# A two-layer hybrid encoder on one core: filler matmuls placed anew, ScalarE's drain points made finer, both layers written out

## Time and profile before

| | us |
|---|---|
| median of 3 runs (lowest, highest) | 3152.52 (3151.27, 3157.33) |
| the profiled execution's own time | 3157.31 |
| its span, first to last instruction | 3155.1 |
| TensorE busy | 2934.4 (93%) |
| VectorE, ScalarE, GpSimd busy | 1583.5, 970.8, 821.5 |
| mean granted TensorE clock | 0.97 of full |

### The profile page before, as it was taken

How to read it: one execution, slowest core, us unless ns; L and a number is a source line. 1 busy time by engine, 2 the same in 40 slices (tenths; PEclk the granted TensorE clock), 3 DMA queues, 4 the chain that set the end, 5 groups by cost and what they waited for, 6 DMA issues and landing times. The chain is left out here.

```text
span 3155.1 us, 46968 instructions
## 1 busy us (share of the span) xinstructions
PE 2934.4 (93%) x18888; PEld 1564.1 (50%) x18888; DVE 1583.5 (50%) x3180; ACT 970.8 (31%) x1836; POOL 821.5 (26%) x572
## 2 busy tenths in 40 slices
PE   6988999999998999999999889999999989999997
PEld 3445554566544465544445364545765444654443
DVE  2477867433379602155216877583334784020743
ACT  2245653211142324300113556522111432253000
POOL 1116312321243232232020353122211423322320
PEclk9998999999999999999999989989999999999998
DMA  5000101100111311263040011011011213112621
GB/s 203 17 27 14 54 14 41 38 32 29 45 64 31 112 65 46 94 206 110 0 141 17 27 37 31 14 40 41 29 32 52 67 38 119 54 44 94 227 77 60
DMA packets 132356, 195.87 MB, mean 62 GB/s; under 512 B 8072, under 2 KB 87976, under 8 KB 131880
## 3 DMA queue, kind: packets, MB, share of 16 engines
q1 hardware_dynamic: 113544, 158.74, 15.5%
q10 hardware_dynamic: 18592, 34.09, 2.9%
HBM read 146.14 MB, written 48.78 MB: 62 GB/s over the span
## 5 line engine op out<-in xcount | busy, mean ns | idle before, releaser
L493 PE MATMUL ps<-hT,wr 128*128 128x512 f32 x1600 | 768.5, 615 | 27.9 <-ACT wr L539 27.9
L493 PEld LDWEIGHTS ps<-hT,wr 128*128 128x128 f32 x1600 | 295.5, 196 | 342.7 <-issue 298.6
L493 PE MATMUL ps<-sums,wr 128*128 128x512 f32 x800 | 381.5, 605 | 3.8 <-ACT xo L548 3.8
L639 POOL TENSOR_TENSOR gts<-gts,wr 128x512 f32<-128x512 f32 x96 | 147.6, 1538 | 620.6 <-ACT wr L539 495.1
L493 PEld LDWEIGHTS ps<-sums,wr 128*128 128x128 f32 x800 | 146.8, 193 | 161.3 <-issue 152.1
L717 PE MATMUL ps<-xo,arena 128*128 128x512 f32 x512 | 220.1, 592 | 0.0
L614 POOL TENSOR_TENSOR wr<-wr 128x512 f32<-128x512 f32 (+1 forms) x56 | 79.7, 1424 | 527.9 <-PE ps L493 409.4
L493 PE MATMUL ps<-wr 128*128 128x512 f32 x400 | 201.2, 629 | 9.2 <-ACT wr L539 9.2
L1099 DVE CUSTOM_DVE_ANT_0 arena<-ps,arena 128x640 f32<-128x640 f32 (+7 forms) x128 | 90.3, 706 | 215.5 <-PE ps L1000 198.1
L1459 DVE TENSOR_SCALAR_CACHE_REDUCE arena<-arena,sm 128x384 f32<-128x384 uint16 (+7 forms) x256 | 192.8, 809 | 2.2
L539 ACT ACTIVATE wr<-ps 128x512 f32<-128x512 f32 x150 | 88.9, 593 | 322.1 <-PE ps L493 289.7
(11 more groups left out here) (313 smaller groups left out, 4767.5 us busy)
## 6 DMA issues: line engine op xcount, KB each, us to landing
wr<-in_w_in SPq DMA_DIRECT2D x68, 1024.0 KB, 5.3
gate_tanh<-gts ACTq DMA_DIRECT2D x128, 256.0 KB, 2.0
arena<-gate_tanh SPq DMA_DIRECT2D x128, 256.0 KB, 3.0
x_cur<-arena SPq DMA_DIRECT2D x2, 4096.0 KB, 23.2
arena<-in_w_branch SPq DMA_DIRECT2D x8, 1024.0 KB, 7.5
wr<-in_w_out SPq DMA_DIRECT2D x8, 1024.0 KB, 6.5
arena<-x_cur SPq DMA_DIRECT2D x4, 2048.0 KB, 9.1
arena<-in_x SPq DMA_DIRECT2D x4, 1024.0 KB, 8.1
```

Of the source, the lines that this page charges most:

```text
L493: ins = pe.matmul(ap, lhsT=right(u, w_side)[:, kt, :], rhs=left(h_side, kt), start=fresh and kt == 0, stop=kt == half_k - 1, skip_group_ch ...
L639: pool.tensor_tensor(dst, dst, stage_of(u), ALU.add).then_inc(sg("pool_added"), 1)
```

## The change

- The filler constants: 70 instead of 49 steps at the end of the search, 4 instead of 3 behind each rotary product of q and k there, 19 instead of 10 before D's sums of squares, one step between D's output transposes (7 in all); in B one call of the added steps is (3, 3, 3, 11) for m = 0 and (3, 3, 3, 11, 3) for m = 1 instead of 20 each, 2 steps before the last local values of each m, and 8 steps and then the rest of the current unit before B's transposes, instead of 16.
- A block by rows may start at an odd place in the queue.
- ScalarE's marks: 10 steps drained before the first bit, a mark after each of the two Signs at 26/5 steps a bit, a drain to step 92 before it waits for bit 16; B's end mark is split in two, one behind the first level's exponential.
- The loop is written out (l = 0, 1); addresses are constants. The first norm runs within layer 0, after a Sqrt on a dummy value; the identity is loaded apart and first, then x, layer 0's parameters, the other constants. TensorE transposes the first four row tiles when they are normed, through six banks. The next layer's parameters are loaded before the branch weights, whose loads stand later in SP's program. In the last layer `final_g` is multiplied within the norm, each row tile is stored at once, and no barrier follows.

The diff without the change of indentation, cut to its core:

```diff
-TOPK_FILL = 49
+TOPK_FILL = 70
+QK_ROPE_FILL = 4
-ROPE_BITS = (4, 5, 6, 7, 11, 12, 13, 14)
+ROPE_BITS = (3, 4, 5, 6, 10, 11, 12, 13)
-D_FILL = {"start": 6, "kk": 10, ...
-B_FILL = {"start": 16, "end": 6, "khn": 2, "adds": 20, "att": 1, "turn": 16}
+D_FILL = {"start": 6, "kk": 19, ...
+B_FILL = {"start": 16, "end": 6, "khn": 2, "adds": (3, 3, 3, 11, 3), "att": 1, "last": 2, "turn": 8}
...
+        for l in range(DEPTH):
+            jobs = Jobs()
...
-                if free and (len(js) == 1 or len(fill_blocks) % 2 == 0):
+                    if free:
...
         def pe_transpose_x(pe):
+                    if l == 0:
+                        pe.wait_ge(sg("rows_normed"), 4 * half + 4)
-                    ap = jobs.open(pe, key, gbank(pe))
+                        ap = jobs.open(pe, key, [G[0], G[1], T, O, S2[0], S2[1]][(KT * half + kt) % 6])
...
+            def pe_fill_unit(pe):
+                while fill_at[0] < len(fills):
+                    pe_fill(pe, 1)
...
             jobs.ready(sp, ("branch", len(tail) - 1))
             sp.dma_start(xin[:, 4:8, :], x_rows[:, 4:8, :]).then_inc(sg("xr2_loaded"), 16)
+                if l + 1 < DEPTH:
+                    sp.wait_ge(sg("next_par_loaded"), 16)
+                else:
+                    sp.dma_start(H(17), final_g).then_inc(sg("f_loaded"), 16)
+                    for n, i in enumerate(pair_rows):
+                        sp.wait_ge(sg("f_scaled"), n + 1)
+                        sp.dma_start(out[0, P * i:P * i + P, :], xo[:, i, :]).then_inc(sg("f_stored"), 16)
...
+                if l + 1 < DEPTH:
+                    sp.dma_start(par[:, :], params[l + 1]).then_inc(sg("next_par_loaded"), 16)
...
-            loads.append((mixer_after["A"], sp_branch_weights))
+                loads.append((("S", "A", 4), sp_branch_weights))
...
-                    dve.tensor_scalar(xo[:, order[i - 2], :], xin[:, order[i - 2], :], inv[:, c], None, ALU.mult)
+                            dve.scalar_tensor_tensor(xo[:, row, :], xin[:, row, :], inv[:, c], H(17), ALU.mult, ALU.mult)\
+                               .then_inc(sg("f_scaled"), 1)
...
-                            beside_search(pe, ROPE_FILL)
+                                beside_search(pe, QK_ROPE_FILL)
...
+                    def beside(k, half):
+                        passed = 13 + (26 * k) // 5 + 2 * half - ropes - 2 * (k >= 10) + 12 * (k >= 16)
+                        act_fills(act, ("beside search", min(passed, searched[0] - 1)))
+                    act_fills(act, ("beside search", 10))
                 for k in range(32):
+                            if k == 16:
+                                act_fills(act, ("beside search", 92))
                     act.wait_ge(sg("cand_ready"), k + 1)
                     for i in act_tiles:
+                            if i == act_tiles[1]:
+                                beside(k, 0)
...
-                    act_fills(act, ("beside search", 14 + (22 * k) // 5 - ropes + 10 * (k // 16)))
+                        beside(k, 1)
...
-                    for n in range(B_FILL["adds"] // 4):
-                        pe_fill(pe, 4)
+                        for n in range(4 + m):
+                            pe_fill(pe, B_FILL["adds"][n])
...
+                            else:
+                                pe_fill(pe, B_FILL["last"])
...
                 pe_fill(pe, B_FILL["turn"])
+                    pe_fill_unit(pe)
...
+                            if n == 0:
+                                act_fills(act, ("B end", m, 0))
...
                     pe_o_turn(pe, "D", i, [o_rows[:, i, 0:P], o_rows[:, i, P:2 * P]])
+                        if i + 1 < NT:
+                            pe_fill(pe, 1)
...
+                    if l == 0:
+                        act.wait_ge(sg("root_table"), 1)
+                        act.activation(root, msq, ACT.Sqrt)
+                        act_norm(act, "first", sg("rows_in"), range(NT))
...
+                        sp.dma_start(con[:, 0:P], consts[:, 0:P]).then_inc(sg("ident_loaded"), 16)
+                        for n in range(4):
+                            sp.dma_start(xin[:, 2 * n:2 * n + 2, :], x_pairs[:, 2 * n:2 * n + 2, :]).then_inc(sg(f"x_in{n}"), 16)
+                        sp.dma_start(par[:, :], params[0]).then_inc(sg("par_loaded"), 16)
+                        sp.dma_start(con[:, P:], consts[:, P:]).then_inc(sg("con_loaded"), 16)
```

More of the change, by code:

```diff
@@ L1321, in pe @@
-                for name, j in (("q", 4), ("k", 5)):
-                    beside_search(pe, QK_FILL, ("C", j))
-                    unit_done(pe, ("C", j))
+                        key = (b, j, m, half)
+                        ap = jobs.open(pe, key, gbank(pe))
+                        for kt in range(KT):
+                            ins = pe.matmul(ap, lhsT=wr[:, n % 2, kt, P * m:P * m + P],
+                                            rhs=hT[:, kt, 512 * half:512 * half + 512], start=kt == 0, stop=kt == KT - 1)
@@ new lines, in pe_proj_t, with pe_fill @@
+                        jobs.filled(ins, key)
+                        behind[2 * m + half](pe)
+                block_done[n] = key
+            fill_at = [0, 0]
+            def pe_fill(pe, n):
+                for _ in range(n):
+                    if fill_at[0] == len(fills) and not next_unit():
+                        return
+                    key, blk, c, p = fills[fill_at[0]]
+                    if unit_at(key) is None:
+                        pe_fill_direct(pe, key, blk, c, p)
+                    else:
+                        pe_fill_product(pe, unit_at(key), key, c, p)
@@ new lines, in pe @@
+                            pe_rope(pe, "qi1", m, half)
+                            pe_fill(pe, ROPE_FILL)
+                    pe.wait_ge(sg("roped"), 2 * len(index_roped))
+                    pe.wait_ge(sg("ki_doubled"), 16)
+                    for n, (i, hp, c, w) in enumerate(index_units):
+                        if n % 2 == 0:
+                            pe_fill(pe, 2 * IDX_FILL)
+                        key = ("I", i, hp, c)
+                        ap = jobs.open(pe, key, S2[n % 2])
+                        for e in range(2):
+                            rows = slice(HD * e, HD * e + HD)
+                            ins = pe.matmul(ap[:, 512 * e:512 * e + w], lhsT=qi[rows, hp, P * i:P * i + P],
+                                            rhs=ki[rows, 0, c:c + w], start=True, stop=True)
+                        jobs.filled(ins, key)
@@ new lines, in pe @@
+                                pe.matmul(o[rows, oc(h)], lhsT=gt_[rows, h, :], rhs=uz[rows, h, HD:], start=h < 2, stop=True,
+                                          skip_group_check=True)
+                            for c in range(2):
+                                rows = slice(CH * c, CH * c + CH)
+                                ins = pe.matmul(o[rows, oc(h)], lhsT=ht_[rows, h, :], rhs=vn[rows, i, HD * h:HD * h + HD], start=False,
+                                                stop=True, skip_group_check=True)
@@ L1779, in pe @@
-                ap = jobs.open(pe, "bonus", O)
-                for i in range(NT):
-                    for m in range(2):
-                        ins = pe.matmul(ap[:, 4 * i + 2 * m:4 * i + 2 * m + 2], lhsT=tmp[:, m, P * i:P * i + P],
-                                        rhs=Pr("rk_sel", 2 * m, 2 * m + 2), start=True, stop=True)
-                jobs.filled(ins, "bonus")
-                for n in range(3):
-                    pe_fill(pe, D_FILL["decay"])
-                    jobs.mark(("decay", n))
```

3275 lines of the change are left out of this document (1622 added, 1653 removed).

## The result

The changed kernel takes **3018.8 us** (median of 4 runs, 3015.9 to 3021.0) against 3152.0 (4 runs): ratio 0.957, 95% interval 0.956 to 0.959. The forecast was 3031, range 3000 to 3072. The profiled executions are 138.3 us apart (spans 3155.1 and 3016.8), since that of before took 5.3 us more than its median; I account for those 138.

The account below looks back on a forecast made before the run. TensorE, busy 2934.4 of 3155.1 us, was taken as the bound, gains lying in its idles, low clock and edges. 46 us a layer, twice 92, plus 29 at the edges made 121 off 3152.5: 3031 us, range 3000 to 3072.

Parts of the forecast that it names:

- Search: Search of C: 8 us shorter while holding 18 us more filler, 26 us a layer, bounds 14 and 32.
- Both waits I take as closed: Search: TensorE's idles of 7.7 us before the first bit and 11.4 before bit 16 vanish.
- D's squares: Nine steps before D's sums of squares win 1.2 us in one layer, 7.7 in the other: 4.5 a layer.
- an idle of 2.38 us that the change does not touch: D's start: this idle stays, with the low-clock stretch behind it in one layer; the squares win 1.2 there.
- D's transposes: Seven steps between D's eight output transposes fill waits for ScalarE's copies: 6.0 - 1.0 = 5.0 us.
- B, 8 forecast by itself: B: steps and split mark fill or close waits, 5.3 + 2.6 us; with D's transposes 13 a layer, bounds 6 and 18.
- Burst before A: Burst before A, 101 to 56 steps: its 2.23 us wait for weights and a short GpSimd wait go, 2.5 a layer.
- Edges: Start 11 us, second layer's start 5.5, end 12.5: together 29, bounds 20 and 34.
- A: Rival: D's low-clock stretch stays away in both layers and the search leaves no idle; about 3012 us, chance 0.09.
- B: Rival: ScalarE becomes the search's limit, TensorE waits at two banks, half of the 26 lost; 3057 us, chance 0.11.
- C: Rival: moved GpSimd adds slow VectorE's chains in D and B, ten collisions of 1.1 us a layer; 3053, chance 0.09.
- D: Rival: the mark between the two Signs stalls ScalarE each search bit, 3.4 us a bit; 3251 us, chance 0.04.

Follow-up runs that it names:

- run 6: Changed kernel with 157 search steps instead of 178 and marks that fit them (22/5 steps a bit, 81 before bit 16): 3049.3 us.
- run 1: Changed kernel with all filler counts and ScalarE marks of search, D and B put back as before; edges and order of filler products stay: 3116.7 us.
- run 2: Changed kernel with the old ScalarE marks in the search, the 21 added steps kept: 3071.2 us.
- run 3: Changed kernel with the 21 added search steps taken out (157), the new marks kept at 26/5 steps a bit: 3101.0 us.
- run 8: Changed kernel with one filler step between each two of B's eight transposes too, seven a layer taken from the burst before A: 3013.3 us.
- run 9: Changed kernel with the seven steps between D's transposes put ahead of the first of them (24 to 31): 3033.0 us.
- run 10: Changed kernel without ScalarE's split mark at B's ends: 3021.0 us.
- run 11: Changed kernel without B's seven added steps, which the fill up to a whole unit puts ahead of B's transposes: 3022.1 us.
- run 4: Changed kernel with nine steps fewer before D's squares (19 to 10), coming only ahead of B's transposes: 3058.5 us.
- run 5: Changed kernel with nine steps moved from before D's squares (19 to 10) to behind them, before the bonus (37 to 46): 3037.6 us.
- run 7: Changed kernel with two more steps before D's squares (21) and two fewer before the bonus (35): 3018.0 us.
- run 12: Changed kernel with 21 steps before D's squares, 35 before the bonus, and a step between B's transposes: 3009.8 us.

## Why the prediction was right, and where it was not

**What bounds the kernel** was read rightly: every gain lies in an idle, a low-clock stretch or an edge of TensorE. The total came out 12 us better than the forecast, within its bounds, by terms that miss in both directions. That it lies so near is partly luck: by the accounting the search brought 6 us less than its term, attention and D's chunks 4 us less, D's squares 7 us more, the edges 4.5 more and the stretch from D's transposes to B's 15 us more, which is outside that term's own bounds of 6 and 18 a layer (19.8 and 21.6).

**Search, 26 forecast, 23 by the accounting.** "Both waits I take as closed" held but for 1.8 us. The length was forecast at 168 and is 171.2: the sum had 4.8 us of waits and 3 of low clock, the trace has 9.6 us of waits (2.23 for weights, the rest of up to 1.8) and no low clock. The z gate's wait of 2.6 us, which the sum kept, is gone. That the filler's marks and not VectorE set the length is shown by run 6 (154.7 us); but VectorE is busy for 137.6 us of it, not 129. Wrong was the thought that the gain is the added steps: run 6 gives 19 (against run 1) to 21 us (against the kernel before) to the marks and about 1.5 to the steps in the search itself. With the 178 steps in place the marks are worth 24 to 27 us (run 2).

**D's squares, 4.5 forecast, 7.4 and 8.2.** The step that failed is "an idle of 2.38 us that the change does not touch". It does: the idle stands in all four kernels with 157 search steps (before, runs 1, 3, 6) in both layers, and in none of those with 178, and each time half clock follows for 13.7 to 17.1 us. I had taken this for chance, by what the Trainium skill says of the monitor's free-running periods (TensorE: Matmul & The Clock Gate, Part 1: The HAM clock gate). Here it was no chance, since the idle itself went; why the search's steps remove it no run shows. Where a short idle stays, the traces fit that page: the wait of 1.86 us before the squares stands in both layers of six kernels (the changed one, runs 2 and 8 to 11), and the clock falls behind it in 2 of the 12. In run 10 it comes 0.4 us earlier than in the changed kernel. Windows of the changed kernel and of run 10:

```profile
501.00:513.00 12.00, 10.12 (x20) 3.78 (x19) 8.44 (x9) 4.41 (x5) 0.00 (x0) 0.86 0.17 65
```

```profile
501.00:513.00 12.00, 9.25 (x21) 3.64 (x21) 9.08 (x9) 4.01 (x4) 1.08 (x1) 1.00 0.18 66
```

Of the 7.4 us some 5.3 lie ahead of the squares and 3.0 between the bonus and the values, where the sum had nothing; 0.7 is lost between them.

**D's transposes, 5.0 forecast**: 5.2 in run 9's first layer, which is right, and 9.6 in its second, where B and the burst add to it.

**B, 8 forecast by itself, about 15.** That the wait of 4.61 us and the slow stretch behind it "go by the split mark" is wrong (run 10), and for the added steps alone, 1.7 + 2.6 in the sum, run 11 shows no gain that can be told. What the sum lacked is that the whole chain from D's transposes to B's is 7 to 9 us shorter. VectorE's rows over that stretch show where: before, and after.

```profile
L1679 DVE TENSOR_TENSOR arena<-arena 128x512 f32<-128x512 f32 x12 | 11.7, 974 | 6.8 <-ACT arena L1608 6.6
...
L1649 DVE SCALAR_TENSOR_TENSOR arena<-arena,sm 128x1024 f32<-128x1024 f32 x2 | 4.6, 2335 | 0.0
```

```profile
L1734 DVE TENSOR_TENSOR arena<-arena 128x512 f32<-128x512 f32 x12 | 8.9, 741 | 0.7 <-ACT arena L1661 0.6
...
L1704 DVE SCALAR_TENSOR_TENSOR arena<-arena,sm 128x1024 f32<-128x1024 f32 x2 | 2.5, 1280 | 0.0
```

VectorE waits 6 us less for ScalarE's exponentials, and single products fell from 2.3 to 1.3 us. Run 1, with the new edges and the old counts, has 9.5 us of that wait in layer 1 and 3.1 in layer 2, and 2.34 us for the same product. The filler's products stand elsewhere beside this chain; that this is worth up to 10 us a layer is shown by runs 4 and 5.

In this stretch VectorE is busy 5.9 and 7.5 us less in the changed kernel, nearly all of what the chain is shorter. The traces show why. VectorE and GpSimd work at the same time there for 57 us before and 53 to 60 in runs 1, 3, 4 and 6, but for 38 to 41 us in the changed kernel and runs 2, 5, 7, 9, 10 and 11 (47 in 8 and 12). What parts the two groups is how far the queue has come at D's transposes: 30 steps further than before in the second (37 in run 9), 21 or fewer in the first. The rows around the long reciprocal, first VectorE's, then GpSimd's, before:

```profile
930.73 12.95 DVE L1646 RECIPROCAL arena<-arena 128x2048 f32<-128x2048 f32 x1
943.72 4.59 DVE L1649 SCALAR_TENSOR_TENSOR arena<-arena,sm 128x1024 f32<-128x1024 f32 x2
...
943.75 1.26 POOL L616 TENSOR_TENSOR wr<-wr 128x512 f32<-128x512 f32 x1
944.97 2.25 POOL L617 TENSOR_TENSOR wr<-wr 128x512 f32<-128x512 f32 x1
```

In the changed kernel:

```profile
914.38 12.95 DVE L1701 RECIPROCAL arena<-arena 128x2048 f32<-128x2048 f32 x1
927.37 2.48 DVE L1704 SCALAR_TENSOR_TENSOR arena<-arena,sm 128x1024 f32<-128x1024 f32 x2
...
923.31 1.26 POOL L660 TENSOR_TENSOR xo<-xo,wr 128x512 f32<-128x512 f32 x1 [2.69 <-ACT wr L560]
```

Before, GpSimd adds during 2.5 us of the reciprocal and then beside the two products. In the changed kernel it adds during 7.4 us of the reciprocal, which takes 12.95 us either way, and the products behind it are free.

**Burst before A** 2.5, measured 2.4 and 2.7: right. **Attention** was taken at nothing and costs 1.3 us a layer.

**Edges, 29 forecast, 33.5 and, by run 1, 35.5.** Start and end were right within 1.2 us. In the second layer the idle before the first transpose fell from 9.23 to 5.13 us, the whole step of 3.5 us and a little more; from there to the projection it takes another 3.6 us less, 2.5 in the sum. The trace does not tell a saved fetch of instructions from a saved barrier, and no run parts them.

**The rivals.** A was half right: the low stretch stays away in both layers, but idles of up to 2.2 us remain in the search. B did not happen: ScalarE is busy 105.5 of 171 us. C's mechanism is real, but with the other sign: in B the change moved the products out of the chain's way. Run 4 loses 10 us a layer beyond the squares, near C's 11, though not by ten collisions of 1.1 us: in D's chunks it is two waits of 2.05 and 2.85 us and the low clock. D did not happen: TensorE waits for ScalarE by no more than 1.8 us at a time in the search.

## What to carry to other kernels

A count of filler is worth what it puts beside each later stage, not only what it fills where it stands: run 4 lost 21 us and run 6 27 us more than the stage in which their steps were cut. Hold the later order fixed when one count is tested (take the steps out here, put them back right behind), and change marks and counts together. An engine that must drain another's banks should do so in small portions ahead of its own wait; here that was worth 19 to 21 us a layer in the search without an added step (run 6), and 24 to 27 with them (run 2).

## What was not expected of the hardware

- VectorE and GpSimd slow each other both ways: a GpSimd addition of 128x512 takes 1.27 us alone and up to 3.3 beside VectorE's 2048-wide products; one VectorE product of 128x256 took 2.00 us instead of 0.42, and those of 128x2048 take 3.24 instead of 2.29. VectorE's reciprocal of 128x2048 takes 12.95 us whether GpSimd adds beside it for 2.5 us or 7.4, and the additions stay at 1.27 us there.
- Behind an idle of 2.38 us the granted clock was 0.50, the level of 1.2 GHz, for 13.7 us or more in both layers of four kernels, while behind one of 1.86 us it fell in 2 cases of 12. Behind idles of 1.86 to 2.3 us it fell for 3.4 us or not at all. The idle's length alone does not set the stretch: behind idles of 2.57 to 3.85 us in the search (before, runs 1, 2, 3, 6 and 7) it fell for 3.4 us, once for 6.8, or not at all. Behind the 2.38 us stand the sixteen low-rank products of 64 rows.
- Eight transposes, each waiting 0.47 us for a copy, ended in a stretch of 6.8 us at half clock where nothing stood between them, in D (run 9, layer 1), in B (changed kernel, layer 1) and all four times in the kernel before; with a step of filler between them, in neither of the two.
